# Two-block transformer kernel: later loads for modulation vector 6, and low parts of weights placed elsewhere in VectorE's order

## The reference

```python
mod = (einsum('bd,dn->bn', silu(c), w_ada) + b_ada).reshape(b, 3, 3, D_MODEL)
h = modulate(x, norm_w[0], mod[0,0], mod[0,1]);  x = x + 0.5*mod[0,2]*swiglu(h, ffn_w13[0], ffn_w2[0])
h = modulate(x, norm_w[1], mod[1,0], mod[1,1])
branches = stack([attention(h), gated_convolution(h)])          # each 256 x 512
merged = sum_g sigmoid(gate_logits_g) * (branches_g @ w_branch_g)
x = x + mod[1,2] * (merged @ w_out)
h = modulate(x, norm_w[2], mod[2,0], mod[2,1]);  x = x + 0.5*mod[2,2]*swiglu(h, ffn_w13[1], ffn_w2[1])
```

## Time and profile before

| | |
|---|---|
| median of 3 runs | 1025.68 us (1024.45 to 1025.98) |
| the profiled execution | 1024.91 us, its span 1023.1 us |
| busy: PE, DVE, ACT, POOL | 98%, 70%, 53%, 4% of the span |
| bytes moved by DMA | 212.26 MB, mean 207 GB/s |

### The profile page before, as it was taken

How to read it: one execution, slowest core, us unless ns; L and a number is a source line. 1 busy time by engine, 2 the same in 40 slices (tenths; PEclk the granted TensorE clock), 3 DMA queues, 4 the chain that set the end, 5 groups by cost and what they waited for, 6 DMA issues and landing times.

```text
span 1023.1 us, 19724 instructions
## 1 busy us (share of the span) xinstructions
PE 1005.1 (98%) x8440; PEld 983.7 (96%) x8440; DVE 716.1 (70%) x1234; ACT 537.2 (53%) x903; POOL 36.1 (4%) x71
## 2 busy tenths in 40 slices
PE   8999999999999999999999999999999999999997
PEld 6899999999999999999999999999999999999997
DVE  3587788978688788867656679655567775555586
ACT  4464444456656455543444577555456465444553
POOL 0121000000000010000000000004000000000000
PEclk9999999999999999999999999999999999999999
DMA  9979888956636673877645457436257565656521
GB/s 336 368 225 359 308 314 304 322 189 218 205 112 196 233 251 103 281 240 243 218 166 196 134 166 223 149 119 182 72 176 229 183 226 186 197 178 204 165 83 42
DMA packets 144480, 212.26 MB, mean 207 GB/s; under 512 B 4276, under 2 KB 121256, under 8 KB 144393
## 3 DMA queue, kind: packets, MB, share of 16 engines
q1 hardware_dynamic: 140032, 198.59, 58.0%
q0 software_dynamic: 4096, 12.10, 3.9%
q10 hardware_dynamic: 264, 0.31, 0.1%
HBM read 209.88 MB, written 1.11 MB: 206 GB/s over the span
## 4 chain that ended last, share of the span: by engine, by line
PE 88%; DVE 8%; ACT 2%; issue 1%; DMA 0%; SPq 0%; DVEq 0%
PE PS L471 86%; DVE wlo L1835 4%; PE PS L479 2%; DVE W L1777 1%; ACT whi L1328 1%; DVE hl L1786 1%; DMA SC<-in_x_dram 0%; DVE xT L1786 0%; DVE W L1786 0%; ACT W L1315 0%; ACT SC L1320 0%; DVE SS L1777 0%; DVE HT L1786 0%; DVE SC L1777 0%; ACT SR L1320 0%
## 5 line engine op out<-in xcount | busy, mean ns | idle before, releaser
L1835 DVE TENSOR_TENSOR wlo<-raw,whi 128x1024 fp32r<-128x1024 f32 (+2 forms) x331 | 385.8, 1185 | 152.5 <-ACT whi L1328 151.9
L1328 ACT ACTIVATE whi<-raw 128x1024 fp32r<-128x1024 f32 (+2 forms) x331 | 332.0, 1023 | 161.6 <-PE PS L471 128.6
L471 PE MATMUL PS<-hh,whi 128*128 128x256 f32 (+1 forms) x1376 | 392.0, 286 | 1.9 <-DVE hl L1786 1.9
L471 PE MATMUL PS<-hh,wlo 128*128 128x256 f32 (+1 forms) x1376 | 387.7, 282 | 0.0
L471 PE MATMUL PS<-hl,whi 128*128 128x256 f32 (+1 forms) x1376 | 387.0, 281 | 0.0
L471 PE MATMUL PS<-SR,whi 128*128 128x256 f32 (+1 forms) x1824 | 328.6, 282 | 3.1 <-DVE xT L1786 1.6
L471 PEld LDWEIGHTS PS<-SR,whi 128*128 128x128 f32 x1824 | 279.9, 188 | 5.9 <-DVE xT L1786 2.4
L471 PEld LDWEIGHTS PS<-hh,whi 128*128 128x128 f32 x1376 | 259.2, 189 | 5.5 <-DVE wlo L1835 2.4
L471 PEld LDWEIGHTS PS<-hl,whi 128*128 128x128 f32 x1376 | 260.2, 189 | 0.4
L471 PEld LDWEIGHTS PS<-hh,wlo 128*128 128x128 f32 x1376 | 259.9, 189 | 0.0
L471 PE MATMUL PS<-SR,wlo 128*128 128x256 f32 (+1 forms) x912 | 256.8, 282 | 0.0
(11 more groups left out here) (188 smaller groups left out, 739.1 us busy)
## 6 DMA issues: line engine op xcount, KB each, us to landing
raw<-in_ffn_w_dram SPq DMA_DIRECT2D x60, 1024.0 KB, 7.2
raw<-in_w_in_dram SPq DMA_DIRECT2D x38, 1024.0 KB, 5.4
raw<-in_w_ff_dram SPq DMA_DIRECT2D x32, 1024.0 KB, 5.3
raw<-in_w_ada_dram SPq DMA_DIRECT2D x20, 1024.0 KB, 6.1
SC<-in_w_ada_dram SPq DMA_DIRECT2D x8, 1024.0 KB, 10.5
SC<-in_w_ada_dram POOLq DMA_DIRECT2D x8, 1024.0 KB, 7.5
raw<-in_w_out_dram SPq DMA_DIRECT2D x8, 1024.0 KB, 5.2
raw<-in_ffn_w_dram SPq DMA_DIRECT2D x7, 768.0 KB, 10.3
```

Of the source, the lines that this page charges most:

```text
L471: return e.matmul(o, l, r, start=start, stop=stop, skip_group_check=True)
L1328: e.activation(hi_part(p), raw_part(p), ACT.Copy).then_inc(*hi_done.up(p.i))
L1835: e.tensor_tensor(lo_part(p), raw_part(p), hi32(hi_part(p)), ALU.subtract).then_inc(*lo_done.up(p.i))
```

## The change

It does three things. The four loads of vector 6 move back by one pair of pieces: A0 stood between b0/b1 and b2/b3 and now stands behind b2/b3, A1 behind r0/r1, A2 behind b4/b5 and A3 behind r2/r3. In DVE's `gated` (used by both gated stages) at most one low part beyond the needed ones goes ahead of stage j, and the rest goes behind m_j. The transpose and the addition for vector 6 move from behind r5 and m7 to between r4 and r5, and to behind m6. In `finish` two low parts may go ahead of x0, none ahead of x1 to x3, one each from x4, where one went ahead of each.

```diff
         self.tall("branch", wb, 0)
-        self.ada(w_ada, 6, 0)
         for j in range(2, 8, 2):
             self.tall("branch", wb, 128 * j)
             if j < 6:
-                self.ada(w_ada, 6, j // 2 + j // 4)
+                self.ada(w_ada, 6, j - 2)
             self.row("out1", a["w_out"][0], j - 2)
-            if j == 2:
-                self.ada(w_ada, 6, 2)
+            if j < 6:
+                self.ada(w_ada, 6, j - 1)
...
                         row(j - 3)
+                        if j == 7:
+                            last_columns()
                         row(j - 2)
-                last_columns()
...
                     opening(j)
+                    if j == 6 and last:
+                        last()
                     on.wait_ge(dve_done, ("mv", key, j))
...
-                    if j == 7 and last:
-                        last()
                     hi_after(("stage", key, j))
...
-            hi_before(("ada_col", 6), 2)
             on.wait_ge(dve_done, ("mod", 6))
...
                 for n in range(8):
-                    lo_for(("acc", key, n), 1)
+                    lo_for(("acc", key, n), 1 if n > 3 else 0 if n else 2)
...
-                    lo_for(("stage", key, j), 99 if j < 7 else 0)
+                    lo_for(("stage", key, j), 1 if j < 7 else 0)
...
                     tt(aring[j % 4][1], w[:, 0:256], hi32(aring[j % 4][0]), ALU.subtract, ("m", key, j))
-
-            gated(1, gate_view, "gate")
-            lo_for(("ada_col", 6), 2)
-            mod_shift(6, 4, 0, ("mod", 6))
+                    if j == 6 and last:
+                        last()
+                    if j < 7:
+                        lo_for(("stage", key, j))
+
+            gated(1, gate_view, "gate", lambda: mod_shift(6, 4, 0, ("mod", 6)))
```

More of the change, by code:

```diff
@@ L2304, in dve_program, with gated @@
             lo_for(("back1", 11))
-            def gated(key, gate, name):
+            def gated(key, gate, name, last=None):
                 for j in range(8):
                     w = W1[:, j % 3, :]
-                    lo_for(("stage", key, j), 99 if j < 7 else 0)
+                    lo_for(("stage", key, j), 1 if j < 7 else 0)
                     after_act((name, j), (name, j + 8))
```

## The result

| | before | changed |
|---|---|---|
| median, us | 1025.29 (1024.37 to 1026.29, 20 runs) | 1026.29 (1025.37 to 1028.68, 20 runs) |
| ratio to before | | 1.0014, 95% interval 1.0008 to 1.0021 |
| the profiled execution, its span | 1024.91, 1023.1 | 1028.68, 1026.9 |

The change costs 1.0 us, within the 2 us that the prediction set as its bound, and 0.4 us above the time forecast. The runs reach 2.4 us above their median, those of before 1.0. The profiled execution was the slowest of all, so it must not be read as typical.

What follows compares the result with a forecast made beforehand. DVE, with ACT in its loop, was taken to bound the first gated stage; terms 0 + 0.55 - 0.3 = +0.25 on 1024.91 gave 1025.2, and 0.77 for the runs' median gave 1025.9 us, range 1024.0 to 1027.8.

Steps and rivals of the forecast that it cites:

- What bounds the kernel: First gated stage and its end: DVE, with ACT in its loop, bounds; accumulator 7 starts at x3 plus 0.53 us.
- Term 1: First gated stage and finish, DVE's new order up to x3: 0 us, from -0.15 to +0.3.
- +2.0 us: First gated stage: A0, formerly free in DVE's idle time, now adds 2.0 us of DVE work behind 340.19.
- 1.6 to 1.9 us won: First gated stage up to x3: DVE's waits for ACT covered by moved work, less about 0.2 us new waits.
- its walk: DVE's instructions added up in the new order through first gated stage and finish, putting x3 at 389.6 against 389.70.
- Term 2: Finish of key 2: h0 waits for ACT behind a later x0, +0.55 us, bounds +0.3 and +0.6.
- Term 3: Finish of key 3: x3 and PE's start come 0.33 us earlier, -0.3 us, bounds -0.4 and 0.
- In this gated stage PE never waits, and the moved low parts have pieces to spare: 0: Gated stage ahead of key 3's finish: moving the low parts there costs 0.
- x0 waits for PE here. The second low part now goes into that wait: Finish of key 3: the second low part fills DVE's wait for PE ahead of x0; x3 comes 0.33 us earlier.
- Term 4: Finish of key 4: h_n come about 0.4 us earlier, but PE is in other matmuls, so 0.
- The rival of the clock: New stalls of 1.5 and 1.7 us: clock falls to 1.2 GHz, 2.87 us more per piece, 1028.8 and up; chance 0.03.
- By the trace a stall of this size costs only itself: New PE stalls in the first gated stage and finish: the clock stays at 2.4 GHz, as behind one 1.60 us stall.

Runs made afterwards that it cites:

- e5: The changed kernel with the loads and sums of vector 6 in the order of before; 1025.11 us, 1.0001 of the kernel before.
- e9: The changed kernel with old finish for keys 1 and 2, old second gated stage and old order of vector 6's loads; 1022.61 us, 0.9976 of the kernel before.
- e10: The changed kernel with the first gated stage's low parts where they were before; 1028.04 us, 1.0027 of the kernel before.
- e2: The changed kernel with finish as it was (at most one low part ahead of every x_n); 1024.54 us, 0.9994 of the kernel before.
- e3: The kernel before with only finish changed; 1025.22 us, 1.0007 of the kernel before.
- e4: The changed kernel with the second gated stage's low parts as before, finish as changed; 1025.71 us, 1.0006 of the kernel before.
- e8: The changed kernel with four more unused DVE additions ahead of x3, to lengthen the stall before accumulator 7; 1029.33 us, 1.0037 of the kernel before.
- e1: The changed kernel with low part u' of the first finish put ahead of x4 instead of x3; 1026.82 us, 1.0016 of the kernel before.
- e6: The changed kernel with finish as it was for keys 1 and 2 and the second gated stage as before; 1023.79 us, 0.9988 of the kernel before.
- e7: The changed kernel with six unused matmuls on PE ahead of the wait before accumulator 7; 1026.13 us, 1.0012 of the kernel before.

## Why the prediction was right, and where not

**What bounds the kernel: right.** The start of accumulator 7 follows x3 by 0.54 us in the changed kernel (391.16 less 390.62), by 0.53 before. e5, e9 and e10 moved DVE's work and time followed, by -1.2, -1.2 and +1.8 us.

**Term 1, DVE's order up to x3 (0): right, and both entries of its balance were tested.** "+2.0 us" for A0 and "1.6 to 1.9 us won" by covered waits gave nought. Measured: 1.3 and 1.8 us (e5, e10), with accumulator 7 at -0.2. The stall of 1.5 us at b6 (1.42), m7 later (accumulator 0 by 0.28, predicted 0.35), x0 earlier by 1.4 (1.46) and the stall ahead of accumulator 7 came as written. A0's later place costs less than its 2.0 us because DVE, when it is that much sooner, must wait for the transpose of vector 6's sum (0.60 us, in e5 and e9). The balance leaves out the change in finish, which only its walk had: undoing it (e2) gives 0.7 us back at accumulator 7. By what each undoing gave, 1.3 - 1.8 + 0.7 = +0.2 stands against the measured -0.2. The 0.4 us between them was not traced, and the move of vector 6's transpose and addition was never undone alone.

**Term 2, finish of key 2 (+0.55): right.** 0.59 in the changed kernel, 0.60 alone (e3). That it would show as a longer stall for h6 was wrong (0.34 us in both).

**Term 3, finish of key 3 (-0.3): wrong by 1.0 in this kernel.** The step that failed is "In this gated stage PE never waits, and the moved low parts have pieces to spare: 0". PE had them to spare, but DVE didn't: m7 came 1.26 us later, by the low parts behind mv6. The step ahead of it, "x0 waits for PE here. The second low part now goes into that wait", was right alone (-0.33 in e3, -0.34 in e4). I spent the one wait of 1.28 us twice, once by name and once without noting it. I had shown neither that wait nor m7 among the rows. With both it could have been worked out. m7 is 1.26 later and the second low part takes 1.14, against 1.28 to spare, so x0 is 1.1 late (measured 1.04). Behind x0 there is a low part less (-1.14), but h0 waits 0.55 for ACT, which g' had covered, and 0.2 us more lie ahead of the third low part. That makes x3 late by 0.65 to 0.7.

**Term 4, finish of key 4 (0): right.** The lag doesn't move behind 804.32.

**The rival of the clock (0.03) came true in part of the executions.** The step that failed is "By the trace a stall of this size costs only itself". One execution with a stall of 1.60 us was too little to say so. Of six profiles with a new stall of 1.4 to 2.9 us ahead of an accumulator of key 1, the clock fell in four (the changed kernel twice, e5, e10) and not in two (e4 with 1.43, e8 with 2.79). Nor did it fall in the two with the 1.60 us of the kernel before (its own and e3), nor ahead of an accumulator of key 1 in any with at most 0.8 us there (e1, e2, e6, e7, e9). Size alone doesn't decide. A stall of 1.42 us stands ahead of b6 in eight profiles, one of 1.39 to 1.40 us ahead of accumulator 7 of key 3 in seven, and behind none of these 15 did the clock fall, where it fell in three of four with 1.43 to 1.45 us ahead of accumulator 7 of key 1. The price was 1.5 us and not 2.87. The Trainium skill, page "TensorE: Matmul & The Clock Gate", section "Why this matters for your kernels", warns of idle gaps between bursts, above a length that it names, as a cause of half clock. All stalls here are shorter than that, so by the page none would have cost anything, and the prediction's reading of it ("By that rule the new stall could cost a piece at half speed") went further than the page. The traces bear out the direction and not the length: the fall came behind stalls of 1.43 to 1.45 us too.

Does the clock explain the wide spread of the changed kernel? e7, which fills the stall and leaves all else, has no run above 1026.9, and 11 of 31 runs of the changed kernel are above it. That speaks for it, though not strongly (at 1027.2 it is none against 7 of 31). A part of the spread is the start's: it makes PE up to 1.5 us late in the profiles of one kernel or another. The split between the two is not settled for single runs without a profile.

**The sum** was +0.25, and the medians say +0.8 to +1.0. Key 3's +1.0 explains it, less key 1's 0.2, and the clock adds to the mean more than to the median. That the time came within 0.4 us of the forecast is in part luck: the three runs of before that it started from had a median 0.39 us above that of all 20.

## What to carry to other kernels

List the slack by its place ("1.28 us ahead of x0"), and take off from it what each edit puts in. Two edits that are both free alone cost when they use the same wait, and undoing either is then a gain. A change of several parts with a sum near nought is worth taking apart: here the low parts behind mv_j in the first gated stage are worth 1.8 us, and the later loads (1.2 to 1.3 lost), finish at keys 1 and 2 (0.7 and 0.6 lost) and the second gated stage (1.0 lost beside the new finish) hid it. These are the lags that undoing each one alone took off the changed kernel. They need not add up exactly. A low part belongs where DVE would wait for ACT, between x0 and x1, and not ahead of both.

## What the runs showed of the hardware

- PE idle for 1.4 us between long busy stretches was enough in three profiles to have the granted clock at 1.2 GHz behind it, for some 3.5 us, and then 2.4 GHz again. The fall begins with the first matmul behind the stall (391.2), some 0.7 us later (390.5 in e5, stall over at 389.87), or 0.4 us ahead of its end, with PE still idle (385.1 in e10, stall of 2.87 us over at 385.51). The same stall at the same place left it at 1.00 in e4, and so did 2.79 us in e8. Fifteen stalls of 1.39 to 1.42 us at two other places left it at 1.00 as well. So it depends on the place, and at one place on chance. Why, no run here tells.
- A fall of the clock behind which PE waits anyway is free (e10: 0.51 us of wait for x3 left at 392.63).
- PE is 0 to 1.5 us late behind the first 25 us from execution to execution, against the profile of before, as much as all that this change does. In the changed kernel and in e4 the wait behind it is for a load (0.96 us at 23.84, 1.50 at 24.32).
